# Softmax shifts by a minimum over negated queries, the selection mask added on TensorE, and low parts of weights in halves

## The reference

```
s = jnp.einsum('bnqhgd,bnkhd->bnhgqk', q, kw).astype(jnp.float32) * scale      # windowed
s = s - slopes[None, None, :, :, None, None] * dist[:, :, None, None]
m = jnp.maximum(jnp.max(s, axis=-1, keepdims=True), sink_l)
e = jnp.exp(s - m)
probs = (e / (jnp.sum(e, axis=-1, keepdims=True) + jnp.exp(sink_l - m))).astype(v.dtype)
```

## Time and profile before

| what | value |
|---|---|
| median of 3 runs | 2875.31 us |
| lowest and highest run | 2872.71 and 2878.05 us |
| time of the profiled execution | 2874.89 us |
| its span, first to last instruction | 2873.0 us |
| mean granted clock of TensorE | 0.983 of full speed |
| "mla", layer 1 and 2 | from 211.6 and from 1140.2 us |
| "gqa", layer 1 and 2 | from 298.5 and from 1228.7 us |
| "dsa" | 2205.1 to 2293 us |
| "mem" | from 2434.5 us |

### The profile page before, as it was taken

How to read it: one execution, slowest core, us unless ns; L and a number is a source line. 1 busy time by engine, 2 the same in 40 slices (tenths; PEclk the granted TensorE clock), 3 DMA queues, 4 the chain that set the end, 5 groups by cost and what they waited for, 6 DMA issues and landing times. The chain is left out here.

```text
span 2873.0 us, 37336 instructions
## 1 busy us (share of the span) xinstructions
PE 2727.7 (95%) x13556; PEld 2193.9 (76%) x13556; DVE 1452.4 (51%) x2215; ACT 1112.2 (39%) x1733; POOL 378.7 (13%) x299
## 2 busy tenths in 40 slices
PE   5999999999999799999999999989898899899998
PEld 4876678988887687667898888767686588788886
DVE  5556654533324655665353332455588636634333
ACT  4345543422224434554342222433633534522221
POOL 1010001311102201000131110320011012311101
PEclk9999999999999899999999999999999999999999
DMA  3321122222232232011322223212232122122222
GB/s 125 128 88 45 33 72 96 81 102 96 94 117 88 69 121 99 30 45 60 106 76 96 102 95 111 88 64 83 74 118 74 59 84 93 40 92 88 102 103 88
DMA packets 37057, 245.96 MB, mean 86 GB/s; under 512 B 4144, under 2 KB 5168, under 8 KB 7984
## 3 DMA queue, kind: packets, MB, share of 16 engines
q1 hardware_dynamic: 33600, 239.09, 23.9%
q10 hardware_dynamic: 3312, 4.93, 0.5%
HBM read 241.91 MB, written 2.10 MB: 85 GB/s over the span
## 5 line engine op out<-in xcount | busy, mean ns | idle before, releaser
L549 PE MATMUL bank<-h_hi,w_hi 128*128 128x512 f32 x2024 | 806.4, 398 | 12.1 <-POOL h_lo L2110 4.7
L551 PE MATMUL bank<-h_hi,w_lo 128*128 128x512 f32 x2024 | 791.1, 391 | 0.0
L550 PE MATMUL bank<-h_lo,w_hi 128*128 128x512 f32 x2024 | 791.0, 391 | 0.0
L1504 DVE TENSOR_TENSOR w_lo<-raw,w_hi 128x2048 fp32r<-128x2048 f32 x153 | 353.4, 2310 | 367.1 <-ACT w_hi L1048 365.7
L549 PEld LDWEIGHTS bank<-h_hi,w_hi 128*128 128x128 f32 x2024 | 381.6, 189 | 105.7 <-issue 19.0
L551 PEld LDWEIGHTS bank<-h_hi,w_lo 128*128 128x128 f32 x2024 | 381.4, 188 | 80.8
L550 PEld LDWEIGHTS bank<-h_lo,w_hi 128*128 128x128 f32 x2024 | 381.9, 189 | 79.7 <-issue 3.4
L1048 ACT ACTIVATE w_hi<-raw 128x2048 fp32r<-128x2048 f32 x153 | 291.9, 1910 | 224.1 <-PE bank L551 217.5
L1516 DVE TENSOR_TENSOR w_lo<-raw,w_hi 128x2048 fp32r<-128x2048 f32 x62 | 142.0, 2292 | 158.0 <-ACT w_hi L1260 156.5
L550 PE MATMUL bank<-a_lo,w_hi 128*128 128x512 f32 x528 | 205.4, 389 | 0.0
L549 PE MATMUL bank<-a_hi,w_hi 128*128 128x512 f32 x528 | 205.4, 389 | 0.0
(11 more groups left out here) (397 smaller groups left out, 4401.0 us busy)
## 6 DMA issues: line engine op xcount, KB each, us to landing
raw<-in_stream SPq DMA_DIRECT2D x226, 1024.0 KB, 4.8
x<-in_xT SPq DMA_DIRECT2D x2, 1024.0 KB, 12.6
out_T<-x ACTq DMA_DIRECT2D x8, 256.0 KB, 2.1
p_f<-in_pT ACTq DMA_DIRECT2D x2, 512.0 KB, 3.9
memf<-in_memT ACTq DMA_DIRECT2D x1, 1024.0 KB, 5.6
cst_sb<-in_cst ACTq DMA_DIRECT2D x1, 411.5 KB, 6.5
pos_i<-in_pos ACTq DMA_DIRECT2D x1, 258.0 KB, 9.1
vec<-in_vec ACTq DMA_DIRECT2D x2, 26.0 KB, 1.7
```

The source lines that it names most:

```text
L549: nc.tensor.matmul(ps, wh, xh, start=start, stop=False)
L550: nc.tensor.matmul(ps, wh, xl, start=False, stop=False)
L551: return nc.tensor.matmul(ps, wl, xh, start=False, stop=stop)
L1504: nc.vector.tensor_tensor(lo[:, :], raw[v % 2][:, :], hi[:, :].bitcast(F32), ALU.subtract).then_inc(lo_ready, 1)
```

## The change

All four attentions take negated, scaled queries: `qc`, `q_a`, `qd` and `mq` are multiplied by minus the scale where they are copied out of their banks (a copy becomes a multiplication by a number, a product with a table takes a second factor). So the bank holds minus the scaled score. DVE takes the minimum of it straight into `st_neg`, `st_max` and its negation (L1714 before) are gone, and ACT's exponential has factor -1 in place of the scale. The bias of "gqa" and the sink change their sign with it.

In "dsa" DVE no longer adds the mask. `leave_out` writes it (now positive) into `hidden`, which has the type of the high parts, and PE adds it: after the scores of items t and t + 1 come two matmuls of a unit matrix with `hidden`, into the same two banks. The minimum and the exponential read the bank. The scores of the next pair wait for `exp_done` of the last item in place of `shift_ready`.

In `after_blocks` the low part of a unit is made in two halves of 128 x 1024 by `split_piece`, the first in the round in which the whole was made, the second one round later, after the reciprocal and the scaling of that round. `lo_ready` comes with the second. Other stages keep `split_unit`.

```diff
-MASKED = -1.0e30
+MASKED = 2.0 ** 100
...
-                    nc.tensor.matmul(SCORES[t % 2][:, 0:len(ks) * P], a["q"](h, b), a["k"](h, ks),
-                                     start=True, stop=True).then_inc(logits_done, 1)
+                    mm = nc.tensor.matmul(SCORES[t % 2][:, 0:len(ks) * P], a["q"](h, b), a["k"](h, ks), start=True, stop="mask" not in a)
+                    if "mask" not in a:
+                        mm.then_inc(logits_done, 1)
+
+                def hide(t):
+                    b = items[t][1]
+                    n = len(a["keys"](b)) * P
+                    nc.tensor.matmul(SCORES[t % 2][:, 0:n], ident_r[:, :], a["mask"][:, b, 0:n], start=False, stop=True).then_inc(logits_done, 1)
...
-                                pe.wait_ge(shift_ready, c.at("I", st, t))
+                                pe.wait_ge(shift_ready if a["biased"] else exp_done, c.at("I", st, t))
                             scores(t)
                             scores(t + 1)
+                            if "mask" in a:
+                                hide(t)
+                                hide(t + 1)
...
-                                             scale=a["scale"], accum_out=st_sum[:, t:t + 1]).then_inc(exp_done, 1)
+                                             scale=-1.0, accum_out=st_sum[:, t:t + 1]).then_inc(exp_done, 1)
...
+            def scale_out(c, st, n, dst, factor):
+                dve.wait_ge(tile_done, c.at("T", st, n + 1))
+                nc.vector.tensor_scalar(dst, ps_of(c, st, n)[:, :], factor, None, ALU.mult).then_inc(tile_free, 1)
...
-                for b in beside(st, t - 2, per) if t >= 2 else ():
-                    if b % BLK == BLK - 1 or b == TILES[st][-1][-1]:
-                        split_unit(c, st, b // BLK)
+                for piece in range(2):
+                    for b in beside(st, t - 2 - piece, per) if t >= 2 + piece else ():
+                        if b % BLK == BLK - 1 or b == TILES[st][-1][-1]:
+                            split_piece(c, st, b // BLK, piece)
+
+            def split_piece(c, st, u, piece):
+
+                v = c.base[st]["U"] + u + 2
+                dve.wait_ge(hi_ready, c.at("U", st, u + 3))
+                at = slice(piece * UC // 2, (piece + 1) * UC // 2)
+                ins = nc.vector.tensor_tensor(w_lo[v % 2][:, at], raw[v % 2][:, at], w_hi[v % 2][:, at].bitcast(F32), ALU.subtract)
+                if piece == 1:
+                    ins.then_inc(lo_ready, 1)
...
-                        link(nc.vector.reduce_max(st_max[:, t:t + 1], src[:, 0:n], AX_X))
-                        nc.vector.tensor_scalar(st_neg[:, t:t + 1], st_max[:, t:t + 1], -a["scale"], None, ALU.mult).then_inc(shift_ready, 1)
+                        nc.vector.tensor_reduce(st_neg[:, t:t + 1], src[:, 0:n], AX_X, ALU.min).then_inc(shift_ready, 1)
...
+                    link(nc.vector.tensor_copy(hidden[:, 0, 0:P], score[:, 0, 0:P]))
+                    link(nc.vector.tensor_copy(ident_r[:, :], ident))
...
-                link(nc.vector.tensor_scalar(score[:, b, 0:w], score[:, b, 0:w], 0.5 * (NEG + TAKEN), MASKED, ALU.is_gt, ALU.mult))
+                link(nc.vector.tensor_scalar(hidden[:, b, 0:w], score[:, b, 0:w], 0.5 * (NEG + TAKEN), MASKED, ALU.is_gt, ALU.mult))
```

More of the change, by code:

```diff
@@ L262, in block_kernel @@
         sq_acc = rstd[:, 1, :]
-        st_max = sb("st_max", 116, [32])
         st_neg = sb("st_neg", 116.25, [32])
@@ L347, in block_kernel @@
         score = ar("score", 0, [ST, S])
+        hidden = ar("hidden", 0, [ST, S], F32R)
+        ident_r = ar("ident_r", 34, [P], F32R)
         merged2 = ar("merged2", 75, [KD, S])
@@ L484, in block_kernel @@
                         o=lambda i: (oc_hi[:, i, :], oc_lo[:, i, :]), per_tile=2),
-            "dsa": dict(heads=8, keys=lambda b: range(b + 1), scale=HD ** -0.5, pT=[pT0_2, pT1], prob=prob2, biased=True,
+            "dsa": dict(heads=8, keys=lambda b: range(b + 1), scale=HD ** -0.5, pT=[pT0_2, pT1], prob=prob2, biased=False, mask=hidden,
                         q=lambda h, b: qd[64 * (h % 2):64 * (h % 2) + 64, h // 2, b * P:(b + 1) * P],
@@ L1322, in evac_uq @@
                     if n < 8:
-                        take_hi(c, "uq", n, n, q_a[0:NOPE, n, :], src=lambda ps: ps[0:NOPE, :])
+                        take_hi(c, "uq", n, n, q_a[0:NOPE, n, :], src=lambda ps: ps[0:NOPE, :], scale=-ATT["mla"]["scale"])
                     elif n < 12:
@@ L1730, in attention @@
                         also(t)
+                if also is not None:
+                    also(len(items) + 2)
                 while taken < a["heads"] // a["per_tile"]:
@@ L1856, in evac_z1 @@
                     else:
-                        copy_out(c, "z1", n, n, qc[:, n - 6, :], lambda ps: ps[:, :], wait_act=False)
+                        scale_out(c, "z1", n, qc[:, n - 6, :], -ATT["gqa"]["scale"])
                 stage_loop(c, "z1", evac_z1)
@@ L1862, in evac_uq @@
                         dve.wait_ge(act_took, c.at("A", "uq", n + 1))
-                        nc.vector.tensor_tensor(q_a[64:P, n, :], ps_of(c, "uq", n)[64:P, :], cs[64:P, :], ALU.mult).then_inc(tile_free, 1)
+                        nc.vector.scalar_tensor_tensor(out=q_a[64:P, n, :], in0=ps_of(c, "uq", n)[64:P, :], scalar=-ATT["mla"]["scale"],
+                                                       in1=cs[64:P, :], op0=ALU.mult, op1=ALU.mult).then_inc(tile_free, 1)
                     elif n < 12:
@@ L1876, in evac_z1b @@
                     if n < 2:
-                        copy_out(c, "z1b", n, 0, qc[:, 2 + n, :], lambda ps: ps[:, :], wait_act=False)
+                        scale_out(c, "z1b", n, qc[:, 2 + n, :], -ATT["gqa"]["scale"])
                     else:
@@ L1884, in alibi @@
                 def alibi(h, b):
-                    return dist[:, b, 0:len(windowed(b)) * P], -(2.0 ** (-8.0 * (h + 1) / HEADS)) * HD ** 0.5
+                    return dist[:, b, 0:len(windowed(b)) * P], 2.0 ** (-8.0 * (h + 1) / HEADS)
                 def add_am(n):
@@ L2022, in evac_z2 @@
                     dst = {8: ki, 22: kk}.get(n)
-                    copy_out(c, "z2", n, 0, qd[:, n - 18, :] if dst is None else dst[:, :], lambda ps: ps[:, :], wait_act=False)
+                    if dst is None:
+                        scale_out(c, "z2", n, qd[:, n - 18, :], -ATT["dsa"]["scale"])
+                    else:
+                        copy_out(c, "z2", n, 0, dst[:, :], lambda ps: ps[:, :], wait_act=False)
                 for t in idx_items(n):
@@ L2084, in evac_mem @@
                     split_unit(c, "mv", (t - 25) // 8)
-            attention(c, "dsa", lambda h, b: (score[:, b, 0:(b + 1) * P], 1.0), also=evac_mem)
+            attention(c, "dsa", also=evac_mem)
             merge(c, 2, "cm", 2)
@@ L2092, in _ @@
                     for g in range(2):
-                        ins = nc.vector.tensor_tensor(mq[:, 2 * p + g, cols(half)], ps_of(c, "mq", 2 * half + p)[:, cols(g)],
-                                                      rstd[:, 0, cols(half)], ALU.mult)
+                        ins = nc.vector.scalar_tensor_tensor(out=mq[:, 2 * p + g, cols(half)], in0=ps_of(c, "mq", 2 * half + p)[:, cols(g)],
+                                                             scalar=-ATT["mem"]["scale"], in1=rstd[:, 0, cols(half)],
+                                                             op0=ALU.mult, op1=ALU.mult)
                     ins.then_inc(tile_free, 1)
```

4 lines of the change are left out of this document (2 added, 2 removed).

## The result

| | before | changed |
|---|---|---|
| median | 2875.39 us (4 runs) | 2852.34 us (4 runs) |
| lowest and highest | 2872.71 and 2878.05 us | 2851.24 and 2853.18 us |
| profiled execution | 2874.89 us | 2852.84 us |
| its span, mean granted clock | 2873.0 us, 0.983 | 2851.0 us, 0.987 |

A later repetition of both kernels (e10) gave 2855.4 against 2873.5, ratio 0.9934 (0.9921 to 0.9948), so the gain is 18 to 23 us.

What follows compares the result with a forecast made beforehand. PE, busy for 95% of the span, was taken as the bound. Savings of 5.4 ("gqa"), 1.2 ("mla"), 0.6 ("mem") and 2 ("dsa") made 9.2 us off 2874.89: 2865.7, predicted as 2866 us, range 2857 to 2873.

Steps and rivals of the forecast that it cites:

- "gqa", both layers: Two 1.46 us stalls a layer shrink to 0.2 by halves and negation; 2.7 us a layer, 5.4 saved.
- "mla", both: Earlier first exponential and end, and no late score behind the second low part: 0.6 us a layer, 1.2 saved.
- "dsa", pairs: Change over the score pairs: +3.9 us at 128 keys, -0.8 at 256, -3.6 at 384, -0.6 at 512.
- "dsa", its end: At the end of "dsa" the last exponential comes earlier by what DVE saves there: -1 us.
- The mask matmuls: New PE work in "dsa": 0.46, 0.35, 0.23, 0.12 us a pair for 512 to 128 keys, 4.7 us in all.
- The wait behind the high part: In "dsa", scores wait for item 9's exponential behind ACT's 1.91 us operation: 128-key pairs 1.3 us longer, three times.
- The rival of the slower round trip over ACT: The round trip over ACT sets every "dsa" pair: at most 1.1 us a pair, 18 us, 2886; chance 0.10.
- that of masks at the scores' rate: "dsa" gives the rest back: for instance mask matmuls at the scores' rate, +7 us; 2870 to 2874; chance 0.22.
- the way over the exponential: In "dsa" at 512 keys, scores through both minima to the last exponential: 4.1 us, pair taken as 4.7 against 4.85.
- The negation: Its removal gives DVE back 0.08 us an item; whoever waits for the shift gets it about 0.19 us earlier.
- the first case: The prediction's own case for the whole kernel: 2860 to 2870 us, chance 0.58.
- opens up: "dsa" pairs come down to PE's own work and the low-clock stretch goes: -9 to -13 us, 2855 to 2859; chance 0.10.

Runs made afterwards that it cites:

- e10: The changed kernel again, unchanged, for a second trace, beside runs of the kernel before: 2855.4 us, ratio 0.9934.
- e6: The changed kernel with the mask added twice to every pair of "dsa": 2858.2 us, ratio 0.9941.
- e7: The changed kernel without the mask matmuls in "dsa": 2849.2 us, ratio 0.9914.
- e2: The kernel before with negated, scaled queries and one minimum for maximum and negation; mask on DVE, whole low parts: 2863.0 us, ratio 0.9955.
- e3: The kernel before with the mask added by PE alone (large negative mask), maximum and negation kept, whole low parts: 2865.0 us, ratio 0.9969.
- e14: The same kernel as e3, run again for a second trace: 2869.9 us, ratio 0.998.
- e5: The changed kernel with whole low parts beside the attentions in place of halves: 2858.2 us, ratio 0.9944.
- e8: The changed kernel with ACT's high part in "dsa" behind the odd item's exponential and DVE's halves one round later: 2851.5 us, ratio 0.9922.
- e15: The changed kernel with the second half of the low parts in "dsa" two rounds behind the first: 2855.6 us, ratio 0.9933.
- e16: e8 with the second half of the low parts two rounds behind the first (rounds 11 and 13, ...): 2855.0 us, ratio 0.9929.
- e1: The kernel before with only the low parts beside the attentions in two halves: 2870.2 us, ratio 0.9981.
- e4: The changed kernel with the mask back on DVE (queries negated, low parts in halves): 2857.6 us, ratio 0.9945.
- e13: The kernel before with two useless float32 matmuls of 384 columns behind "gqa" in each layer: 2872.3 us, ratio 0.9991.
- e11: The changed kernel with 20 useless 128x512 matmuls in PE's wait ahead of "dsa": 2855.5 us, ratio 0.9941.

## Why the prediction was too small

Most of its mechanisms are the ones that the trace shows. It was 10 to 13 us short on the traces. Some 7 of these lie in a term that it put at nothing, the granted clock outside "dsa", and 3 to 5 in "dsa".

| step | predicted | measured on distances |
|---|---|---|
| "gqa", both layers | 5.4 | 5.7 and 5.8; parts 2.1 (halves) and 0.7 (negation) a layer |
| "mla", both | 1.2 | 0.9 |
| "mem" | 0.6 | 0.9 |
| "dsa", pairs | 1.1 | 5.9 (first traces) and 4.9 (second) |
| "dsa", its end | 1 (with the pairs taken as 2) | 1.35 and 0.2 |
| rest, mostly granted clock | 0 | 7.2 and 7.0 |
| sum | 9.2 | 22.0 and 19.7 |

**What held.** The stall of 1.46 us became 0.39 with the half and nothing with both; the second half made nobody in "gqa" late; no wait for the later `lo_ready` is seen there; halves take 1.22 us. The mask matmuls cost 4.4 us over fifteen pairs, 4.2 by the prediction's rate (its 4.7 has the sixteenth), and are on the path in all but the first (e6, e7). The wait behind the high part makes the 128-key pair 1.1, 1.2 and 0.9 us longer (1.3 predicted). The 256-key pair is at -0.24 and -0.26 in two rounds (-0.2 predicted) and at 0 in the last. The rival of the slower round trip over ACT is refuted, as is that of masks at the scores' rate.

**What failed in "dsa".** Three steps.

- "The pairs of one round of blocks start 3.89, 4.77, 5.23 and 4.85 us apart" was used as if all four rounds were like it. It is the shortest round: 18.7 us, against 20.6 and 21.6 for the two before it, and the fourth has a 384-key pair of 6.34. What the change brings the 384- and 512-key pairs down to, 3.7 to 5.0 and 4.5, I had about right (4.3 to 5.1, and 4.7); what they came from I had wrong. At 384 keys it is 0.5, 1.8, 1.5 and 1.8 us less, not four times 0.9, and at 512 keys 0.3, 1.3 and 0.35, not 0.15. Of the 1.3, 0.95 us is the drop of the earlier trace rows.
- "PE's own work in that pair was 4.85 - 1.23 = 3.6 us" took the wrong bracket. A bracket tells of idle time ahead of its row, so the 1.23 us belong to the 384-key pair; the 512-key pair ends with the 0.77 us at 2266.05. Its own work is 4.85 - 0.77 = 4.1 us, with the masks 4.5. That is what the changed kernel takes, with no idle time: PE sets this pair, not the way over the exponential that the prediction put at 4.7.
- The negation, "0.19 earlier" for whoever waits, is 0.38 for a pair that hangs on the second shift (e2). With the mask on DVE it alone takes 4.3 us off "dsa", and the mask on PE alone 3.9. Together they are 4.9 to 5.9, not 8.2. Both shorten DVE's part of the pair, and at 512 keys either alone takes it near what PE needs: 4.47 us with the negation (0.39 of it a wait), 4.66 with the mask on PE, 4.50 with both, of which the masks are 0.46. The sum for the stage had no term of its own for the negation.

**What failed in the sum.** "Clock ... is in the width of the first case", and other stages were costed at nothing. The mean granted clock went from 0.983 to 0.987, second traces 0.982 to 0.985. By the record of the clock in the traces that is 12 and 10 us of lost clock fewer (1 minus the granted clock, over the span, idle time of PE included): 5.1 and 1.7 in "dsa", 7.0 and 8.4 elsewhere, where the distances leave 7.2 and 7.0. It has two sources:

- In "dsa" the change itself raises it. Ten traces without the mask on DVE and with waits of PE left alone (e3, e14, changed twice, e5, e6, e7, e8, e15, e16) have 0.93 to 0.96 in that stretch, and six with it (before twice, e1, e2, e4, e13) 0.89 to 0.92, whatever the shift. The drop of the earlier trace rows at 2241 to 2248 stood behind 2.12 us of waiting ahead of the 512-key pair; with the mask on PE that wait is 0.96 (e3), 0.57 or nothing, and the changed kernel has 1.00 from 2211 to 2268 (the granted clock is the third value from the end):

```profile
2211.00:2231.00 20.00, 18.54 (x145) 14.12 (x144) 11.65 (x31) 11.31 (x30) 0.00 (x0) 1.00 0.15 53
2231.00:2268.00 37.00, 34.61 (x231) 21.80 (x229) 21.50 (x56) 21.53 (x58) 0.00 (x0) 1.00 0.16 58
```

  This is the rival "opens up", in its clock if not in its price. In time it is worth less than in clock, as e11 shows; on the pairs' distances most of it is already counted.
- In stages that the change does not touch, drops come and go with the moment (e13) and with the execution (e3 and e14). The kernel before has the lowest mean clock of all kernels here, 0.9825, with e1 next to it at 0.9829. The shift of e13 alone raised it by 0.002, about 5 us by the estimate above. So the 7 us need no merit of the change to explain them: all that follows in it is earlier by what the attentions save. That this is the cause is not shown, for no run has the changed kernel's parts without their shift. They do belong to the kernel and not to luck of one trace, since they are there in both and in the mean of all executions. The Trainium skill (TensorE: Matmul & The Clock Gate, What's actually happening) has the clock follow from how busy the array recently was, which fits the drops behind waits; which waits are followed by one and which not, no run here explains.

None of e8, e15 or e16 beats the changed kernel by more than the runs can tell.

## What to carry to other kernels

Before one stretch stands for all of its kind, list the others: sixteen pair starts were one reading, and the round chosen was the one with the least to win. Charge a wait to the interval that it ends, not to the one that starts behind it. Two remedies for the same busy engine do not add; their sum ends where the next engine's own work begins, here PE's 4.5 us. And where a kernel is within half a per cent of its form, compare distances between landmarks and the granted clock of all executions, not medians alone: 2.6 us of useless work made this one no longer.

## What the runs showed of the hardware

A drop of the granted clock moves the time of this program by some 1.5 us, and executions of one kernel differ by up to 13 us with it (of e1: 2861.25 us at 0.986 to 2873.58 at 0.982). Two matmuls of a unit matrix with 512 columns cost 0.46 us behind scores that use half of the rows, the same as among matmuls of their own kind. A negation of 0.15 us in a chain costs 0.19, and twice that where two items stand in a row. Fillers in a wait raised the clock of the 130 us around and behind it from 0.93 and 0.95 to 0.99 in one trace and 0.96 in another, and left the time as it is where other engines set the pace.
